# A transformer block with windowed and neighbourhood attention: scores from rounded parts and remainders two heads ahead, and a reordered front

## The reference

```
mod = silu(c) @ w_ada + b_ada            # six vectors of 1024: shift, scale, gate, twice
h   = modulate(rmsnorm(x, g_pre_mix), sh1, sc1);  hc = the same of ctx with mod_c
qa, ka, va, qb, kb, vb = split(h @ w_in) # 8 heads A (2 key heads), 8 heads B, 64 wide; w_in is 1024 x 2304
oa  = softmax([band |q-k| <= 128, context, sink]) @ v       # heads A, rotary on qa and ka
ob  = softmax([8 x 16 neighbourhood + rpb bias, context]) @ v  # heads B
x   = x + ga1 * rmsnorm(concat(rmsnorm(oa), rmsnorm(ob)) @ w_out)
x   = x + ga2 * rmsnorm(top-4-of-32 clamped-SwiGLU experts(modulate(rmsnorm(x), sh2, sc2)))
```

## Time and profile before

| | |
|---|---|
| time, median of 3 runs | 3116.22 us (3113.05 to 3123.14) |
| profiled execution, its own time | 3115.47 us |
| its span from the first to the last instruction | 3113.8 us |
| granted TensorE clock, mean over the span | 0.943 |
| busy: PE, DVE, ACT, POOL | 2715.1, 1847.0, 1475.0, 518.6 us |
| front, up to PE's last projection | 0 to 454.2 us |
| attention, from PE's first transposes | 474.8 to about 950 us |
| middle, and experts and combine | to about 1300, and to 3113.8 us |

### The profile page before, as it was taken

How to read it: one execution, slowest core, us unless ns; L and a number is a source line. 1 busy time by engine, 2 the same in 40 slices (tenths; PEclk the granted TensorE clock), 3 DMA queues, 4 the chain that set the end, 5 groups by cost and what they waited for, 6 DMA issues and landing times. The chain is left out here.

```text
span 3113.8 us, 39558 instructions
## 1 busy us (share of the span) xinstructions
PE 2715.1 (87%) x12534; PEld 2008.5 (65%) x12535; DVE 1847.0 (59%) x2805; ACT 1475.0 (47%) x1743; POOL 518.6 (17%) x447
## 2 busy tenths in 40 slices
PE   3899988998995871599999999999999999999980
PEld 0245576777773440477777777777777777777760
DVE  0430004454442226577777787777777787799977
ACT  0101014555551110456666566666666566677761
POOL 1000002211311114210111011110211022122210
PEclk8999999999997885799999999999999999999995
DMA  9810014224223210777887788778887788799988
GB/s 236 288 43 27 14 41 105 53 49 91 55 45 114 81 68 21 262 254 275 299 284 260 264 290 299 268 251 280 299 285 254 269 291 294 269 370 373 372 307 313
DMA packets 299629, 647.26 MB, mean 208 GB/s; under 512 B 13874, under 2 KB 15170, under 8 KB 299426
## 3 DMA queue, kind: packets, MB, share of 16 engines
q1 hardware_dynamic: 277622, 574.30, 54.5%
q0 software_dynamic: 21968, 72.44, 7.0%
HBM read 606.18 MB, written 46.59 MB: 210 GB/s over the span
## 5 line engine op out<-in xcount | busy, mean ns | idle before, releaser
L1372 DVE TENSOR_TENSOR w_lo_x<-wring_x,w_hi_x 128x2048 fp32r<-128x2048 f32 x446 | 1015.3, 2285 | 58.8 <-issue 32.6
L1286 ACT ACTIVATE w_hi_x<-wring_x 128x2048 fp32r<-128x2048 f32 x448 | 849.8, 1908 | 8.1 <-DMA wring_x<-in_w_mlp 7.6
L1518 PE MATMUL psum<-w_hi_x,x_hi_x 128*128 128x512 f32 x1184 | 497.2, 420 | 3.9 <-DVE w_lo_x L1372 3.2
L1520 PE MATMUL psum<-w_hi_x,x_lo_x 128*128 128x512 f32 x1184 | 463.5, 391 | 0.0
L1519 PE MATMUL psum<-w_lo_x,x_hi_x 128*128 128x512 f32 x1184 | 463.1, 391 | 0.0
L1249 POOL TENSOR_TENSOR poolgate_x<-poolgate_x 128x1 f32<-128x1 f32 x74 | 75.2, 1017 | 1180.9 <-DVE y_x L1405 671.3
L1518 PE MATMUL psum<-w_hi_x,a_hi_x 128*128 128x512 f32 x592 | 249.9, 422 | 15.2 <-DVE a_lo_x L1433 15.0
L1518 PEld LDWEIGHTS psum<-w_hi_x,x_hi_x 128*128 128x128 f32 x1184 | 224.8, 190 | 48.0 <-DVE w_lo_x L1372 8.6
L1520 PEld LDWEIGHTS psum<-w_hi_x,x_lo_x 128*128 128x128 f32 x1184 | 223.0, 188 | 49.1
L1519 PEld LDWEIGHTS psum<-w_lo_x,x_hi_x 128*128 128x128 f32 x1184 | 224.0, 189 | 42.9
L1520 PE MATMUL psum<-w_hi_x,a_lo_x 128*128 128x512 f32 x592 | 231.3, 391 | 0.0
(11 more groups left out here) (285 smaller groups left out, 3932.2 us busy)
## 6 DMA issues: line engine op xcount, KB each, us to landing
wring_x<-in_w_mlp SPq DMA_DIRECT2D x448, 1024.0 KB, 5.7
ring<-in_w_ada SPq DMA_DIRECT2D x12, 2048.0 KB, 9.3
bias<-bias_d SPq DMA_DIRECT2D x16, 1280.0 KB, 14.8
yg<-y_d SPq DMA_DIRECT2D x8, 2048.0 KB, 10.9
ring<-in_w_in SPq DMA_DIRECT2D x4, 2048.0 KB, 8.6
xin<-in_x SPq DMA_DIRECT2D x8, 512.0 KB, 4.9
ring<-in_w_out SPq DMA_DIRECT2D x2, 2048.0 KB
mix_d<-o SPq DMA_DIRECT2D x8, 512.0 KB, 7.1
```

The costliest lines, as they stand in the source:

```text
L1286: act.activation(w_hi[:, n % HI, k, :], ring[:, n % RING, k, :], ACT.Copy).then_inc(hi_done, 1)
L1372: dve.tensor_tensor(w_lo[:, n % LO, k, :], ring[:, n % RING, k, :], w_hi[:, n % HI, k, :].bitcast(F32), ALU.subtract).then_inc(lo_done, 1)
L1518: pe.matmul(bank, hi[:, k, :], w_hi[:, n % HI, k, :], start=False, stop=False)
L1520: last = pe.matmul(bank, lo[:, k, :], w_hi[:, n % HI, k, :], start=False, stop=(k == KD - 1))
```

## The change

**Scores.** `kaT` and `kbT` become f32r tensors with one plane per key head: partitions 0 to 63 hold the key rounded to f32r, partitions 64 to 127 what the rounding left (`key_part`). The query tile stands in `qh` rounded, on both halves of the partitions, and in `ql` as remainder on both halves. A score is then two f32r matmuls (`qh`, `ql`) over 128 partitions that add up in PSUM, in place of one f32 matmul. In the front ACT copies a key group's two heads rounded, DVE subtracts for the remainders; in attention ACT copies the queries (`queries`, four operations of 64 partitions by 512 for each of groups A and B in a tile) and DVE subtracts (`remainders`, four of the same size). POOL no longer touches queries.

**Order in attention.** PE does `transposes(s)`, then `scores(s+2)`, then `values(s-1)`; the last two turns of a tile make the first two scores of the next, whose queries are made at `s` of 7 and 8. ACT and DVE do `evacuate(s)` and then head `s+2`. One square root a tile for both groups (`roots`), with the scaling `norm`, is done in the next tile. The bias is loaded and masked in halves of four heads.

**Front.** Only 4 units of `w_ada` go through `ring` first, with the tokens' loads between them (all ten tiles have buffers of their own, in memory that `v` and `qaT` take later). The other 8 units come as 32 pieces of 512 KB (two chunks each) in `late`, loaded behind the first two units of `w_in`, and DVE multiplies and adds them (`late_piece`, two operations of 128 x 512 a piece, two pieces after each group from the third on); PE sums over the partitions (`sum_late`, eight f32 matmuls). `hT` is made half on DVE, half on ACT, and tiles 4 to 9 between the first groups of the projection, which are in another order of units (2, 3, 4, 0, 1). The columns of the modulation come from small transposes on PE in place of a store to HBM and a load. POOL's queue starts `perm`, `cosT`, `sinT`, the zeros and the bias table only when the last tile of tokens is loaded.

The diff, cut to what is spoken of:

```diff
--- before.py
+++ after.py
-                    self.ka = qkv("kaT", [P, SEQ + CTX])
+                    self.ka = qkv("kaT", [P, NKVA, SEQ + CTX], F32R)
...
-                    self.kb = qkv("kbT", [P, NHB // 2, SEQ + CTX])
+                    self.kb = qkv("kbT", [P, NHB, SEQ + CTX], F32R)
...
+        EARLY = 4
+        LATE = 6 * D // UNIT - EARLY
+        PIECE = 2
+        PIECES = LATE * (KD // PIECE)
...
+        def key_part(g, half, part):
+            _, kind, j, _, hf, width = groups[g]
+            cols = slice(hf * UNIT, hf * UNIT + width)
+            return K.ka[part, half, cols] if kind == "ka" else K.kb[part, 2 * j + half, cols]
...
+            load_unit(0)
             load_x(0)
             load_x(1)
...
+            load_unit(3)
+            for t in range(6, T + TC):
+                load_x(t)
+            load_unit(4)
+            load_unit(5)
+            for m in range(PIECES):
+                load_late(m)
+            for n in range(6, EARLY + 5):
+                load_unit(n)
...
+            pool.wait_ge(x_loaded[T + TC - 1], 16)
...
+            def late_piece(m):
+                u, c = divmod(m, KD // PIECE)
+                dve.wait_ge(late_loaded[m % 2], 16 * (m // 2 + 1))
...
+                        ins = dve.scalar_tensor_tensor(acc, w, cT[:, k:k + 1], acc, ALU.mult, ALU.add)
...
+                for m in range(2 * (g - FIRST_PIECE), 2 * (g - FIRST_PIECE) + 2):
+                    if 0 <= m < PIECES:
+                        late_piece(m)
...
+            def sum_late(u):
+                pe.wait_ge(partial_done, u + 1)
+                pe.matmul(ps[0:LATE, 6, :], unit_of[:, u, :], partial[:, u % 2, :], start=(u == 0), stop=(u == LATE - 1)).then_inc(partial_summed, 1)
...
+            def load_biases(i):
+                first = [sp.value_load(tiles[0:1, bass.ds(i * TCOLS + 2 + half, 1)], min_val=0, max_val=BROWS - LBR - 15 * (NHB - 1)) for half in range(2)]
+                load_bias(i, 0, first)
+                sp.wait_ge(bias_ready, 2 * i + 2)
...
+                load_bias(i, 1, first)
...
+                if s < NHA:
+                    kt = K.ka[:, s // (NHA // NKVA), :]
+                    parts = ((slice(128, 512), kt[:, bass.ds(k_a, LA)]), (slice(512, 768), kt[:, SEQ:]))
+                else:
+                    kt = K.kb[:, s - NHA, :]
+                    parts = ((slice(0, 512), kt[:, bass.ds(k_b, 512)]), (slice(512, 640), kt[:, bass.ds(k_b + 512, 128)]), (slice(640, 896), kt[:, SEQ:]))
+                for to, kv in parts:
+                    for q in (qh, ql):
+                        last = pe.matmul(flat[:, to], q[:, s, :], kv, start=(q is qh), stop=(q is ql))
+                last.then_inc(s_done, 1)
...
-                scores(0)
                 for s in range(NH):
-                    if s + 1 < NH:
-                        scores(s + 1)
...
                     transposes(s)
+                    if s + 2 < NH:
...
+                        scores(s + 2, k_a, k_b)
+                    else:
...
+                        scores(s + 2 - NH, k_next, None)
                     if s >= 1:
                         values(s - 1)
                 values(NH - 1)
...
+            def queries(first, start):
+                for half in range(2):
+                    part, heads, source = q_part(first, half)
+                    for to in range(2):
+                        last = act.activation(qh[HD * to:HD * to + HD, heads, :], source[part, :, bass.ds(start, P)], ACT.Copy)
+                last.then_inc(q_high, 1)
...
                 for s in range(NH):
-                    probs(s)
-                    if s >= 1:
-                        evacuate(s - 1)
...
+                    evacuate(s)
+                    probs((s + 2) % NH, i * NH + s + 2)
+                    if s == 2:
+                        act.wait_ge(s_done, i * NH + 2)
+                        queries(NHA, i * P)
+                    if s == NHA - 1:
+                        act.wait_ge(s_done, i * NH + NHA)
+                        queries(0, next_start)
...
+                    if s == NHA - 2:
+                        roots(2 * i + 1)
...
+            def remainders(first, start):
+                for half in range(2):
+                    part, heads, source = q_part(first, half)
+                    for to in range(2):
+                        last = dve.tensor_tensor(ql[HD * to:HD * to + HD, heads, :], source[part, :, bass.ds(start, P)], qh[part, heads, :].bitcast(F32), ALU.subtract)
+                last.then_inc(q_low, 1)
...
                 for s in range(NH):
+                    evacuate(s)
...
+                    mask((s + 2) % NH, i * NH + s + 2, link)
...
+                    if s == NHA + 1 or s == NH - 3:
+                        dve.sem_inc(bias_free, 1)
+                    if s == 3:
+                        dve.wait_ge(q_high, 2 * i + 2)
+                        remainders(NHA, i * P)
+                    if s == NHA - 1:
+                        norm(i, link)
                     if s == NHA:
+                        dve.wait_ge(q_high, 2 * i + 3)
+                        remainders(0, next_start)
```

More of the change, by code:

```diff
@@ L555, in load @@
[L555 to L559 removed]
+                    src = bass.AP(tensor=src.tensor, offset=(first[half] + RPB_R * HEADS * part) * GRID_W, ap=[[BROWS * GRID_W, GRID_W], [RPB_R * GRID_W, HEADS], [1, LB]])
+                    sp.dma_start(bias[GRID_W * half:GRID_W * (half + 1), HEADS * part:HEADS * part + HEADS, :], src).then_inc(bias_loaded[part], 16)
@@ L566, in _ @@
             pool.memset(zeros[:, :], 0.0).then_inc(zeros_set, 1)
-            pool.memset(qz[:, :, :], 0.0).then_inc(zeros_set, 1)
             pool.dma_start(sink[:, :], io["sink_a"].to_broadcast([P, NHA])).then_inc(sink_loaded, 16)
-            pool.wait_ge(zeros_set, 2)
-            pool.wait_ge(tiles_loaded, 16)
-            def queries(first, source, start, ready):
-                for half in range(2):
-                    part = slice(HD * half, HD * half + HD)
-                    heads = slice(4 * half, 4 * half + 4) if first == 0 else slice(NHA + half, NH, 2)
-                    last = pool.tensor_copy(qz[part, heads, :], source[part, :, bass.ds(start, P)])
-                last.then_inc(ready, 1)
@@ L580, in _ @@
[L580 to L594 removed]
+            pool.sem_inc(bias_ready, 2)
@@ L595, in _ @@
+            with pool.Fori(0, T) as i:
+                pool.wait_ge(mask_b_loaded, 16 * i + 16)
+                for part in range(2):
+                    pool.wait_ge(bias_loaded[part], 32 * i + 32)
+                    rows = bias[:, HEADS * part:HEADS * part + HEADS, :]
+                    pool.tensor_tensor(rows, rows, mask_b[:, :].rearrange("p (a n) -> p a n", a=1).to_broadcast([P, HEADS, LB]), ALU.add).then_inc(bias_ready, 1)
+                pool.wait_ge(bias_ready, 2 * i + 4)
             pool.wait_ge(sink_loaded, 16)
-        def keys(s):
-            return LA + CTX if s < NHA else LB + CTX
@@ new lines, in norm @@
+            def norm(i, link):
+                dve.wait_ge(rms_done, i + 1)
+                link(dve.reciprocal(stat[:, 2, :], stat[:, 1, :]))
+                for g in range(2):
+                    last = dve.tensor_scalar(o[:, g, :], o[:, g, :], stat[:, 2, g:g + 1], None, ALU.mult)
+                last.then_inc(o_done, 1)
+            dve.wait_ge(q_high, 1)
+            dve.wait_ge(tiles_loaded, 16)
+            remainders(0, 0)
+            setup(dve.memset(o[:, :, :], 0.0))
+            setup(dve.memset(stat[:, :, :], 1.0))
```

539 lines of the change are left out of this document (312 added, 227 removed).

## The result

The changed kernel takes **3006.48 us**, median of four runs (3005.02 to 3019.72), against 3115.88 us for the kernel before (four runs); the ratio is 0.9654, 95% interval 0.9641 to 0.9667. The forecast was 2966 us in a range of 2925 to 3015: faster, as forecast, but 40 us short of it. The profiled execution has a span of 3003.3 us, 110.5 less than before where 149.5 was forecast.

What follows compares the result with a forecast made beforehand. PE bounds projection and mostly attention, while the front waits for DMAs. From 3115.5 us, 85 for the front and 65 for attention (8 tiles of 51.1 us, rounded) come off: 2966 us, range 2925 to 3015.

Steps and rivals of the forecast that it cites:

- The front: Before attention: first projection matmul at 60 us, last projection ending at 369 instead of 454.2, 85 us gained (70 to 93).
- The late pieces: In the projection: 32 pieces costed at nothing, with some 30 us of cover before the third unit of `w_in` is wanted.
- Rival 2: Front starts late: zeros and askew write get under `w_in`'s first unit or pieces use up their cover; 2994 us, 7%.
- PE's work in attention: Per attention tile: shorter scores (head B 0.90 us, head A 0.57) cut PE's work from 52.9 to 43.1 us.
- The 128-column pair: In head B's score pass: two 128-column f32r matmuls take 0.22 us together; over 0.4 would show the forecast wrong.
- The waits: Per attention tile: PE waits 6.5 us, about 2 around s=4 and 4.5 at s=8 and 9, none at the seam.
- DVE's sum at s=4: Around s of 3 and 4: DVE has 6.3 us of work, PE 4.4, so PE waits about 2 us.
- The clock: In attention: slower clock behind waits costs 1.5 us a tile; a clock of 0.95 or more expected.
- I add 1.5 us a tile: In attention: allowance for the clock falling behind waits of nearly 3 us, from five transposes taking 1.27 instead of 0.76.
- the bias halves cost nothing: In attention: halves free at s of 9 and 13, wanted at 6 and 10 next tile, some 38 us later; cost nothing.

Runs made afterwards that it cites:

- f_gate: Kernel after without POOL's wait for the last input tile, so its constants, zeros and askew write start at once: 3088.8 us, ratio 0.989.
- q_low_pool3: Kernel after with only the queries' remainders moved from DVE to POOL, the copies left on ACT: 3022.5 us, ratio 0.9703.
- q_skip: Kernel after with queries and remainders made once ahead of the loop and left out of the tiles: 2906.6 us, attention 402.9 against 473.2.
- q_pool: Kernel after with the queries' copies and remainders both made by POOL, group B's between the halves of the bias addition: 2946.4 us, ratio 0.9461.
- pe_fill3: Kernel after with idle transposes of the identity on PE ahead of the waits at s=4, 8 and 9: 2992.4 us, ratio 0.9606.
- b_noadd: Kernel after with POOL's bias addition cut to eight columns of one head for each half: 2919.7 us, attention 471.2 against 473.2.
- q_quarter: Kernel after with the queries' eight copies and eight subtractions a tile spread one a step instead of four in a row: 3024.0 us, ratio 0.9714.
- r_skip: Kernel after with attention's square root replaced by a linear function, needing no other table: 2987.9 us, attention 475.9 against 473.2.
- q_pool_first3: Queries and remainders on POOL, group B's ahead of both halves of the bias addition: 2967.9 us, ratio 0.9533 to the kernel before.
- b_heads: Kernel after with each half of the bias addition as four POOL instructions, one a head: 3011.1 us, ratio 0.9663 to the kernel before.

## Why the prediction was right, and by how much it was off

**The front.** Right, at 88 us instead of 85. The first projection came at 54.5, not 60, since the loads ran at 389 GB/s, not 308. The last ended at 366, 311.5 later, where 309 was forecast. The late pieces cost PE nothing, as forecast: the third unit of `w_in` was issued at 178.6 and PE waited for none. Rival 2 didn't come about, because the askew write fell where PE had its weights; `f_gate` shows what it costs where it doesn't, 39 us with the zeros and constants.

**PE's work in attention.** A little too small: 43.1 forecast, 44.4 to 44.6 of busy time in tiles at clock 1.00. The step was the score passes: head B takes 1.00 us, not 0.90, and head A 0.67 (566.52 to 567.19), not 0.57. The 128-column pair was not the reason: from 578.80 to 578.97 it takes 0.17 us, where I took 0.22. The pair of 512 columns took 0.54 instead of 0.46 (the first of it 0.31 to the next start, not the 0.23 of the earlier trace rows) and that of 256 took 0.29 instead of 0.23: the rate of a long stream of equal matmuls doesn't hold at the start of a pass. By busy time 10 us.

**The waits.** Placed right, and near in size: 57.1 us of idle time are 7.1 a tile against 6.5, 5 us in all, and 6.2 in the six tiles that repeat (the rest is the stall of 5.63 and its like). They stand at s=4 (1.9), s=8 (0.7 to 1.3) and s=9 (2.5 in six tiles, 0.9 in two); at the seam 0.7 to 1.0 is left, where none was forecast. The cause was half right. The forecast had PE wait at s=4 for DVE's remainders, and at s=8 and 9 for ACT and for a part of DVE's work. Each of the waits at s=4, 8 and 9 is released by ACT's copy: at s=4 and 9 it stands behind the four copies of queries, at s=8 behind the root and its table load. `q_low_pool3` has no remainders on DVE and still waits 1.93 at s=4 and 2.54 at s=9. That DVE's sum at s=4 gave the right 2 us is luck. `q_skip` and `q_pool` take the lumps of both engines away; what is left is 1.3 at s=8, the roots, and 0.7 at the seam.

**The clock.** The term that was mis-sized, "I add 1.5 us a tile". PE's busy time is 48.9 a tile, 44.4 at full clock: 4.5 us a tile, 3.0 more than forecast, 24 of the 40 us. The only row behind the 1.5 was one fall at the old seam, five transposes in 1.27 us for 0.76, and how 1.5 follows from it isn't said; behind a wait the clock is at its lower level for a whole head (from 584.31 to 589). `pe_fill3` gives 17 us of attention back by work in the gaps; `q_skip` removes most of the waits and the clock is 0.96 to 1.00. The forecast had looked for 0.95 or more in attention; it was 0.92. Sum of the shortfall in attention: 10 + 5 + 24 = 39, against 39.8 measured (448.6 - 8 x 51.1). This is a division of the time, not three causes: in the two tiles whose clock fell at s=8 the wait at s=9 is 1.6 us shorter, and they take 53.8 us at 0.91, hardly more than the 53.2 of a tile at 0.97. By place, the six tiles that repeat, 54.3 us each, make 19.5 of the 39.8; the other 20 lie in the stretch up to 471.3 and behind 797.4, which take 122.5 us where the forecast has two tiles, 102.2.

**What the forecast had left out.** That the bias halves cost nothing was argued from when a half is wanted, not from what its addition does to DVE while it runs. In the kernel after that hits two tiles, and `b_noadd` shows it to be worth 2 to 4.5 us there; the stalls went, and the next tile ran slower. That it hits only two is luck of phase: `f_gate`, `q_quarter`, `r_skip`, `q_pool_first3` and `q_low_pool3` have it in half of the tiles or more, at 7 to 8 us a tile where it can be told (`f_gate`, `r_skip`). Why the clock falls further in one tile (0.90) than in the next (0.97), with the same instructions, stays open.

## What to carry to other kernels

Price a wait of TensorE at its length and what the clock takes behind it; here the second was over half of the first (4.5 us a tile beside 7.1), and cheap work in the gap gave part of it back. Work in lumps on an engine whose next instruction the bottleneck waits for belongs on an idle engine, if it doesn't delay what that engine owes: moving 16 instructions a tile to GpSimd gained 60 us; moving the eight subtractions alone lost 16, because ScalarE's lumps stayed and GpSimd's additions then fell on VectorE's small operations. And before saying that a GpSimd operation is hidden, look at which VectorE instructions with two SBUF inputs can fall under it, for a change elsewhere moves them there.

## What the runs showed that I had not expected

VectorE instructions with both inputs in SBUF stand still until GpSimd's current addition ends: 128 x 8 elements in 4.06 us instead of 0.156, ending 0.03 us behind it, and such stalls came in ten of the other twelve kernels changed from it (not in `b_noadd` and `q_pool`), in some only once. Those with one input in PSUM ran on beneath it (the mask of 0.88 us at 392.46, within POOL's 391.37 to 402.57). The row of before that shows it was there to be found: `sinkd`, of 0.17 us elsewhere in that kernel, took 1.11 at 495.47 and ended at 496.58, with POOL's addition (485.52 and 11.04 long: 496.56). From before:

```profile
495.47 1.11 DVE L762 TENSOR_TENSOR sinkd<-sink,negm 128x8 f32<-128x8 f32 x1 [0.77 <-ACT S L674]
```

The Trainium skill (SBUF — State Buffer, section Who interferes with whom) has the rule: the port pair that the two engines share is an exclusive lock, and a VectorE instruction with two SBUF inputs contends with a GpSimd instruction that reads SBUF. That the second one blocks for the whole instruction it says of VectorE's two-port modes; these traces show it for two inputs as well (0.03 us between the ends). `b_heads` adds that between two instructions of GpSimd VectorE gets its turn.

While the askew write of 930 KB ran, all queues together moved 98 to 102 GB/s though units were under way (`f_gate` and before); without it they moved 389 (4.5 to 54.5 us of after). In after it took as long, 27.9 us against 30.8 and 31.6. The 33 GB/s of 68 to 87 us there don't tell what it does to others, since SP had no load to issue.
